# DeltaNet layer of a decoder trunk: squares of k from the diagonal of K K^T on VectorE, an earlier Q K^T, and the next unit's remainders split up among the levels

## The reference, cut to what matters

```python
qkv = silu(causal_conv4(h @ w_in))                 # q, k, v: 8 heads of 128
q = l2_normalize(q) * DK**-0.5;  k = l2_normalize(k)   # t * rsqrt(sum(t*t) + eps)
L = exp(where(causal, decay_i - decay_j, -inf))
A = where(strict, (k * beta) @ k.T * L, 0)         # per chunk
U, W = triangular_solve(I + A, [v * beta, k * beta * exp(decay)])
Aqk = where(causal, q @ k.T * L, 0)
# then per chunk: v_new = U - W S;  o = q_dec S + Aqk v_new;  S = cd * S + k_dec.T v_new
o = rmsnorm(o) * norm_w * silu(z);  out = o @ w_out
```

## Time and profile before

| | us |
|---|---|
| runs | 1051.48, 1052.98, 1052.96; median 1052.96 |
| the profiled execution | 1051.15 |
| its span, first to last instruction | 1049.4 |
| PE busy / DVE busy / ACT busy | 1029.4 / 600.6 / 532.1 |
| the DeltaNet stage in the span | about 660 to 845 |

### The profile page before, as it was taken

How to read it: one execution, slowest core, us unless ns; L and a number is a source line. 1 busy time by engine, 2 the same in 40 slices (tenths; PEclk the granted TensorE clock), 3 DMA queues, 4 the chain that set the end, 5 groups by cost and what they waited for, 6 DMA issues and landing times.

```text
span 1049.4 us, 14314 instructions
## 1 busy us (share of the span) xinstructions
PE 1029.4 (98%) x5290; PEld 868.3 (83%) x5290; DVE 600.6 (57%) x812; ACT 532.1 (51%) x808; POOL 51.0 (5%) x112
## 2 busy tenths in 40 slices
PE   8999999999999999999999999999999999999997
PEld 7888888876888888888888888997997978888886
DVE  5645555566564544545555454687597666554543
ACT  7444343547554434436344353587568555543532
POOL 0000000101000000000000000403202200000000
PEclk9999999999999999999999999999999999999999
DMA  9765555433346564563655565433153157555521
GB/s 326 237 200 161 195 214 192 155 136 96 105 135 228 160 215 184 202 199 120 216 184 169 213 216 179 149 104 119 41 181 121 42 169 236 176 173 211 213 83 41
DMA packets 124303, 175.73 MB, mean 167 GB/s; under 512 B 7361, under 2 KB 97761, under 8 KB 124257
## 3 DMA queue, kind: packets, MB, share of 16 engines
q1 hardware_dynamic: 121552, 172.77, 48.8%
q10 hardware_dynamic: 2704, 2.33, 0.7%
HBM read 174.02 MB, written 1.06 MB: 167 GB/s over the span
## 4 chain that ended last, share of the span: by engine, by line
PE 86%; DVE 6%; ACT 5%; issue 2%; DMA 1%; SPq 0%; ACTq 0%; DVEq 0%
PE bank L1565 26%; PE bank L1567 26%; PE bank L1566 26%; PE bank L1896 2%; PE bank L1629 2%; ACT w_hi L695 1%; PE bank L1890 1%; DVE v_T L1381 1%; PE bank L1586 1%; ACT Y L929 1%; PE bank L1799 1%; PE bank L1769 1%; DMA x_sb<-in_x 1%; DVE w_lo L1076 1%; DVE k_T L1381 0%
## 5 line engine op out<-in xcount | busy, mean ns | idle before, releaser
L1076 DVE TENSOR_TENSOR w_lo<-w_raw,w_hi 128x2048 fp32r<-128x2048 f32 x155 | 352.5, 2292 | 143.1 <-ACT w_hi L695 143.0
L695 ACT ACTIVATE w_hi<-w_raw 128x2048 fp32r<-128x2048 f32 x155 | 293.9, 1918 | 111.9 <-PE bank L1567 111.9
L1565 PE MATMUL bank<-w_hi,xT_hi 128*128 128x512 f32 x784 | 309.6, 395 | 1.4 <-DVE w_lo L1246 1.1
L1567 PE MATMUL bank<-w_hi,xT_lo 128*128 128x512 f32 x784 | 305.7, 390 | 0.0
L1566 PE MATMUL bank<-w_lo,xT_hi 128*128 128x512 f32 x784 | 305.3, 389 | 0.0
L1565 PEld LDWEIGHTS bank<-w_hi,xT_hi 128*128 128x128 f32 x784 | 147.2, 188 | 32.6 <-issue 1.9
L1567 PEld LDWEIGHTS bank<-w_hi,xT_lo 128*128 128x128 f32 x784 | 147.1, 188 | 31.1
L1566 PEld LDWEIGHTS bank<-w_lo,xT_hi 128*128 128x128 f32 x784 | 147.3, 188 | 29.5
L748 ACT ACTIVATE silu_g<-bank,rstd 128x256 f32<-128x256 f32 x88 | 36.9, 471 | 247.6 <-PE bank L1567 247.5
L1565 PE MATMUL bank<-w_hi,hT_hi 128*128 128x512 f32 x352 | 138.3, 393 | 0.0
L1567 PE MATMUL bank<-w_hi,hT_lo 128*128 128x512 f32 x352 | 137.2, 390 | 0.0
(11 more groups left out here) (287 smaller groups left out, 966.2 us busy)
## 6 DMA issues: line engine op xcount, KB each, us to landing
w_raw<-in_ffn_w_gate_up SPq DMA_DIRECT2D x170, 512.0 KB, 4.7
w_raw<-in_ffn_w_down SPq DMA_DIRECT2D x88, 512.0 KB, 4.0
w_raw<-in_gdn_w_in SPq DMA_DIRECT2D x32, 512.0 KB, 4.4
w_raw<-in_attn_w_in SPq DMA_DIRECT2D x12, 512.0 KB, 4.2
w_raw<-in_attn_w_out SPq DMA_DIRECT2D x8, 512.0 KB, 3.7
w_raw<-in_gdn_w_out SPq DMA_DIRECT2D x8, 512.0 KB, 4.2
w_raw<-in_ffn_w_gate_up SPq DMA_DIRECT2D x12, 256.0 KB, 5.6
x_sb<-in_x SPq DMA_DIRECT2D x4, 256.0 KB, 4.4
```

Source lines behind the costliest of these rows:

```text
L695: act.activation(w_hi[u0 % RING][:], w_raw[u0 % RING][:], ACT.Copy).then_inc(hi_ready, 1)
L1076: dve.tensor_tensor(w_lo[u0 % RING][:], w_raw[u0 % RING][:], w_hi[u0 % RING][:].bitcast(F32), ALU.subtract).then_inc(split_ready, 1)
L1565: pe.matmul(out_ap, a[0], b[0], start=start, stop=False, **kw)
L1567: return pe.matmul(out_ap, a[1], b[0], start=False, stop=stop, **kw)
```

## The change

1. ACT no longer squares k. DVE multiplies K K^T (in its bank) with the identity for each tile and head (8 instructions per group, result into v_beta, which is free at that point), with the sum of each row accumulated into `sc[:, 1]`.
2. DVE's order: unit 7's split goes behind A; the sums of v's conv go behind Aqk; unit 8's split becomes four pieces of 512 columns, one each in levels n = 0 to 3.
3. PE: q's transposes go between v's two units. Q K^T goes ahead of unit 7 and into banks 2 and 3. The waits for v's sums and z's silu go from before the levels and n = 0 to the start of n = 1; Y at n = 0 waits for Aqk.
4. Unit 8's tiles in the levels go block of the contraction by block (`by_quarters`), each behind the remainder's piece that it reads.

```diff
-KK_BANK, QK_BANK = [2, 3], [6, 7]
+KK_BANK, QK_BANK = [2, 3], [2, 3]
...
 # ACT
                 act.activation(spare[:], norm_cols[:, 0:1], ACT.Sqrt)
-                for t in range(TT):
-                    squares(g, FILL_K + t, 1, kq_ssq)
                 act.wait_ge(kq_inv, g + 1)
...
 # DVE
+            def split_lo_part(u0, j):
+                at = slice(j * BANK, (j + 1) * BANK)
+                dve.wait_ge(hi_ready, u0 + 1)
+                dve.tensor_tensor(w_lo[u0 % RING][:, at], w_raw[u0 % RING][:, at], w_hi[u0 % RING][:, at].bitcast(F32),
+                                  ALU.subtract).then_inc(g_piece_lo if j < 3 else split_ready, 1)
...
-                for n in range(6, 8):
-                    split_lo(U_GDN + 8 * g + n)
+                split_lo(U_GDN + 8 * g + 6)
                 conv_scale(g, 2)
+                for t in range(TT):
+                    dve.wait_ge(KK_psum, TT * g + t + 1)
+                    for h in range(HG):
+                        z = dve.scalar_tensor_tensor(v_beta[:, t, h, :], bank[KK_BANK[t]][:, h * P:(h + 1) * P], 1.0,
+                                                     ident[:], ALU.mult, ALU.mult, accum_out=sc[:, 1, t, h:h + 1])
+                    z.then_inc(kq_ssq, 1)
...
                     z.then_inc(A_ready, 1)
+                split_lo(U_GDN + 8 * g + 7)
...
-                conv(g, 2)
-                split_lo(U_GDN + 8 * g + 8)
                 for t in range(TT):
                     dve.wait_ge(QK_psum, TT * g + t + 1)
                     dve.tensor_tensor(Lm[t]..., bank[QK_BANK[t]][:], Lm[t]..., ALU.mult).then_inc(Aqk_ready, 1)
+                conv(g, 2)
...
+                    if n < 4:
+                        split_lo_part(U_GDN + 8 * g + 8, n)
...
 # PE
+            def by_quarters(u0, banks, part):
+                for m in part:
+                    j, h = m // HG, m % HG
+                    z = products(bank[banks[h // 2]][:, (h % 2) * SEQ:(h % 2 + 1) * SEQ],
+                                 ring(u0, slice(j * BANK + h * P, j * BANK + (h + 1) * P)),
+                                 (xT_hi[:, j, :], xT_lo[:, j, :]),
+                                 start=(j == 0 and h % 2 == 0), stop=False, skip_group_check=True)
+                    if m == 4 * HG - 1:
+                        z.then_inc(unit_done, 1)
...
                     m = 2 * (n - 1) + behind
-                    channel_unit(U_GDN + 8 * (g + 1), 0, CONV_BANKS[g + 1][0], None, range(m, m + 1))
+                    pe.wait_ge(g_piece_lo, 3 * g + m // HG + 1)
+                    by_quarters(U_GDN + 8 * (g + 1), CONV_BANKS[g + 1][0], range(m, m + 1))
...
-                    channel_unit(u, 0, CONV_BANKS[g][0], None, range(EARLY_Q, 4 * HG))
+                    wait_split(pe, u)
+                    by_quarters(u, CONV_BANKS[g][0], range(EARLY_Q, 4 * HG))
...
-                pe.wait_ge(conv_ready, 3 * g + 1)
-                for t in range(TT):
-                    g_transposes(g, t, lambda t, h: q_T[:, h, tile[t]])
                 if g == 0:
                     pe.wait_ge(gate_dve, GATE_G + 2)
                     pe.wait_ge(cum_ready, 1)
-                for kh in range(2):
-                    channel_unit(u + 4 + kh, kh, CONV_BANKS[g][2])
+                channel_unit(u + 4, 0, CONV_BANKS[g][2])
+                pe.wait_ge(conv_ready, 3 * g + 1)
+                for t in range(TT):
+                    g_transposes(g, FILL_Q + t, lambda t, h: q_T[:, h, tile[t]])
+                channel_unit(u + 5, 1, CONV_BANKS[g][2])
...
+                for t in range(TT):
+                    heads(QK_BANK[t], lambda h: q_T[:, h, tile[t]],
+                          lambda h: k_T[:, h, tile[t]]).then_inc(QK_psum, 1)
                 in_unit(u + 7, 0, 1, (0, 1))
...
-                pe.wait_ge(conv_sum, HG * (3 * g + 3))
-                for t in range(TT):
-                    heads(QK_BANK[t], lambda h: q_T[:, h, tile[t]],
-                          lambda h: k_T[:, h, tile[t]]).then_inc(QK_psum, 1)
                 for n, b in enumerate(LEVELS):
+                    if n == 1:
+                        pe.wait_ge(conv_sum, HG * (3 * g + 3))
+                        pe.wait_ge(z_silu, TT * (g + 1))
                     for t in range(TT):
+                        if n == 0:
+                            pe.wait_ge(Aqk_ready, TT * g + t + 1)
...
                     if n == 0:
                         for t in range(TT):
-                            pe.wait_ge(Aqk_ready, TT * g + t + 1)
                             g_transposes(g, FILL_AQK + t, lambda t, h: Lm[t][:, h, :])
-                        pe.wait_ge(z_silu, TT * (g + 1))
```

More of the change, by code:

```diff
@@ L377, in build @@
         X_odd = sem("X_odd")
+        g_piece_lo = sem("g_piece_lo")
         cum_psum = sem("cum_psum")
```

## The result

| | kernel before | changed kernel |
|---|---|---|
| median of 6 runs each, us | 1052.38 | 1056.66 |
| lowest to highest | 1051.48 to 1053.06 | 1055.69 to 1058.45 |
| profiled execution | 1051.15 | 1055.69 |
| its mean granted clock | 0.999 | 0.996 |

The ratio is 1.0045, interval 1.0033 to 1.0057: slower by 0.45%, 4.7 us (the two medians lie 4.3 apart). The forecast was 1056.9 in a range of 1053.4 to 1061.0.

The account below looks back on a forecast made before the run. PE is busy 98%, but before the levels DVE's v sums and ACT's silu, split and XT bound it. Terms +1.97, +2.40 and 0.3 gave +4.7 us, added to the runs' average 1052.1 and rounded up: 1056.9, range 1053.4 to 1061.

Parts of the forecast that it names:

- K K^T later: PE before the squares: q's transposes paid later plus one matmul switch; 0.6 us later in group 0, 0.7 in group 1.
- no wait for k_dec: PE at A's transposes: waits for k_dec, 2.8 us in two before, vanish; none over 0.2 us left.
- in one piece for XT: PE at the transposes of Aqk: waits some 3.7 us at once, where before it waited 0.26.
- the two uncovered waits: PE at v's first unit: waits for banks 6 and 7 in group 0, unit 4's split in group 1.
- the squares: DVE's eight squares of k per group: 0.35 us each, 2.8 in all; scales 0.98 earlier in group 0, 0.55 in group 1.
- the sum: Z starts later behind v's sums, silu, split and XT: +1.97 us in group 0, +2.40 in group 1.
- The clock falls in the new wait: Rival, PE's XT wait: clock drops to 1.2 GHz, up to 2.2 us per fall; 1059.1 or 1061.3; chance 0.15.
- The row that I read for it: Span's end: last matmul ends 1043.13, clock 1.00 to 1046.5, so it falls some 3.6 us behind.
- The argument against it: Against the clock's fall: at span's end no matmul came any more; here some can fall just outside the wait.
- Pieces in the levels: DVE's pieces of unit 8's split: group 1's hole at n = 3 is too short, about 0.3 us lost once.
- From scales to the end of v's sums: DVE: unit 7's split (2.20) and Aqk (1.19) now stand in this stretch, adding 3.39 us.
- The rival of the other sign: Transposes of Aqk: PE's order decides, waits for k_dec, k_w, XT, silu, q_T go; about -4, 1048; chance 0.09.

Follow-up runs that it names:

- experiment 1: Changed kernel with DVE taking the sums of v's conv ahead of Aqk again; 1051.86 against 1051.44, ratio 1.0006.
- 2: Changed kernel with ACT's split of unit 9 moved from before the copies XT to behind level n = 3; 1050.45 against 1051.44, ratio 0.9991.
- 3: Changed kernel with unit 9's split behind level n = 3 and copies XT ahead of ACT's wait for v's sums; 1048.81 against 1051.44, ratio 0.9974.
- experiment 8: Changed kernel with q's transposes back ahead of v's two units on PE; 1057.05 against 1051.15, ratio 1.0049.
- 6: Kernel before with copies XT ahead of ACT's wait for v's sums and unit 9's split at level 3; 1052.29 against 1051.15, ratio 1.0011.
- 11: Changed kernel with unit 7's split back behind unit 6's, ahead of v's scaling and the squares; 1055.45 against 1051.17, ratio 1.0038.
- 5: Kernel before with only k's squares moved to DVE, behind the splits of units 6 and 7 and v's scaling; 1049.85 against 1051.15, ratio 0.9988.
- 10: Changed kernel, q's transposes ahead of v's units, XT and z's silu ahead of ACT's wait for v's sums, unit 9's split at level 3; ratio 0.9956.
- 12: Kernel before, squares on DVE, XT and z's silu ahead of ACT's wait for v's sums, unit 9's split at level 3; 1048.44 against 1051.17, ratio 0.9975.
- run 66: Not a label but a count: the unchanged kernel before, run 66 times beside the experiments; 1050.6 to 1052.1 us in 55 of them.

## Why the prediction was right, and where not

**The direction and its reason** held at every joint: K K^T later by 0.47 and 0.59 (forecast 0.6 and 0.7), no wait for k_dec, PE waiting 3.62 us in one piece for XT (forecast 3.7), the two uncovered waits of 0.40 and 1.49 ahead of v. That the wait's length agrees so well is in part luck: PE came to it at 724.85, the 0.34 us taken off, and not at 725.7, and XT was early against the forecast by about as much. Experiments 1 to 3 moved the chain at three places and the time followed each.

**The term that was mis-sized** is the squares. "I take 0.35 each, 2.8 in all": they took 0.21 each, 1.74 in all, less than the lower bound of 0.27 that I had from A's own instructions. That bound was the mistake. A (L1456 before, L1467 in the changed kernel) takes its scalar from a column, the squares have the constant 1.0 in its place; whether this is the difference was not tried by itself. The accumulator's read of 0.08 us lies beside the next square, which starts as it does. So the scales came 1.1 us earlier in each group than forecast, v's sums were 0.9 and 0.8 less late, and the chain lost about 2.5 us where the sum had 4.4 (1.97 and 2.40). The term enters once per group, so an error of 1 us in it was 2 of the 4.7.

**What made the number right again** was luck: a rival came true as well. "The clock falls in the new wait" got 0.15 and 1059.1 for one fall; it happened in group 0 of the profiled execution, and by the mean clocks each of the six had a fall. Its price was put at up to 2.2 us a fall and is 1.27 here, 2.10 for the longer one of experiment 8. The row that I read for it was right: 3.6 us from the last matmul to the fall at the span's end, and a wait of the same length here. The argument against it, that some matmul can fall just outside, was no argument. The Trainium skill's page "TensorE: Matmul & The Clock Gate" (the table of why this matters for your kernels), which advises against idle gaps between bursts of matmuls, agrees with the fall behind 3.6 us, and made this rival more likely than I did. The falls behind shorter waits in experiments 6 and 11 go beyond that advice. So forecast and rival are not alternatives: the chain makes the gap, the gap takes the clock. A chain of about 2.5, 1.3 for one fall and 0.3 for the pieces make 4.1, the stage's 4.12.

**The other terms.** Pieces in the levels: forecast 0.3, in group 1. From the first X of group 1 to the copy of O it was 19.62 us before (809.92 to 829.54) and 19.94 after (814.06 to 834.00): 0.32. From scales to the end of v's sums 3.62 us were added, forecast 3.39; the difference is the second tile's X, 0.84 us for 0.65, while POOL packed A beside it (its cause was not tried). The Trainium skill's sentence on accumulator outputs ("VectorE: DVE Perf Modes", two Vector instructions with no wait between them) holds: DVE shows a read of its own behind each square, 0.083 us each.

**The rival of the other sign**, that PE's order decides, is refuted by 1 and 2, which leave PE's order as it is and get the loss back. Its figure, 1048, is about where the kernel goes when the place it named is cleared (3: 2.7 us under the kernel before). It decided "when v's sums end by about 722.5"; it was enough to take XT out from behind them.

## What to carry to other kernels

A list of waits says where an engine stands, not what would be next, so before work is moved ahead on one engine, follow the buffer's copy at the next stop back through the other engines' queues. If the queue of the copying engine holds an instruction that the copy doesn't need (here silu of v and a weight split ahead of XT), reorder that first: the rest of this change went from a loss of 6.3 us of the stage, the falls included (8 against 5), to a gain of 2.2 by it (10 against 12). PE's waits are no free slack either: behind the one of 3.6 us TensorE's clock halved, which added 1.27 us to the chain's loss, and with two short ones in its place (experiment 1) it stayed full in the profiled execution. Short waits are no guarantee, as experiments 6 and 11 show.

## What the runs showed of the hardware that I had not expected

A square with an accumulated row sum costs DVE 0.21 us per 128x128 from PSUM (16 instructions of 0.285 us, 16 accumulator reads of 0.083), less than A's 0.27 with a column operand in place of the constant.

A fall of the clock cost 1.27 us in a stretch of small transposes and matmuls that hang on one another, and one that lasted about twice as long 2.10 (experiment 8). It isn't bound to waits of 3.6 us: it came behind one of 2.06 (experiment 11), behind waits of about 1.6 and 0.4 with four transposes between them and behind one of 1.4 in the attention (experiment 6), and, by the mean clock, in a few executions of the kernel before. Whether it comes differs from one execution to the next, and a good part of what a kernel's runs scatter by goes with it: the kernel before, run 66 times beside the experiments, takes 1050.6 to 1052.1 us at 0.998 and 0.999 (55 times), 1051.4 to 1053.3 at 0.996 (7), and 1053.1 to 1053.4 at 0.995 (4).
